# First tile of the norm after a sandwich norm made by VectorE from three prepared tiles, with six filler products in place of ten

## The reference

```python
def rmsnorm(x, gain):
    xf = x.astype(jnp.float32)
    var = jnp.mean(xf * xf, axis=-1, keepdims=True)
    return (xf * lax.rsqrt(var + RMS_EPS) * gain.astype(jnp.float32)).astype(x.dtype)

# first block
    h = rmsnorm(x, norm_mix_pre[l])
    ...
    x = x + rmsnorm(merged @ w_out[l], norm_mix_post[l])      # site "mixpost"
    h = rmsnorm(x, norm_ffn_pre[l])                           # site "ffnpre0"
    f = conv_ffn(h, ffn_w_up[l], ffn_conv_w[l], ffn_conv_b[l], ffn_w_down[l])
    x = x + rmsnorm(f, norm_ffn_post[l])                      # site "ffnpost"
# second block
    x = x + fox_mixer(rmsnorm_2(x, fox_norm[layer]), ...)     # site "fox"
```

## Time and profile before

| what | us |
|---|---|
| median of 3 runs | 2171.79 (2171.71 to 2172.0) |
| the profiled execution | 2171.54 |
| its span, first to last instruction | 2169.7 |
| TensorE busy in the span | 2159.0 |
| VectorE, ScalarE, GpSimd busy | 1210.2, 896.0, 963.7 |

### The profile page before, as it was taken

One profiled execution on the slowest core, in us unless ns is written; L12 is line 12 of the kernel. 1 busy time (PEld: TensorE's weight loads), 2 busy tenths in 40 slices (PEclk: granted clock), 3 DMA queues, 4 the chain that ended last, 5 costly groups with the idle time before them and its releaser, 6 DMA issues.

```text
span 2169.7 us, 26119 instructions
## 1 busy us (share of the span) xinstructions
PE 2159.0 (100%) x10371; PEld 1769.6 (82%) x10374; DVE 1210.2 (56%) x1721; ACT 896.0 (41%) x1405; POOL 963.7 (44%) x741
## 2 busy tenths in 40 slices
PE   9999999999999999999999999999999999999998
PEld 6887788878888878877888888888888888888887
DVE  4975424478996127775566661177676325666511
ACT  5225522354343234675533332265444434333322
POOL 4434345555565435322554444444222254444442
PEclk9999999999999999999999999999999999999999
DMA  5222223333332323211233333322211233333332
GB/s 185 78 68 68 74 83 98 99 95 98 97 98 92 97 74 106 68 50 61 95 98 97 98 95 97 99 95 69 64 56 51 66 101 92 97 97 97 96 97 89
DMA packets 59098, 191.77 MB, mean 88 GB/s; under 512 B 6592, under 2 KB 8800, under 8 KB 58976
## 3 DMA queue, kind: packets, MB, share of 16 engines
q1 hardware_dynamic: 58976, 190.09, 28.0%
HBM read 187.96 MB, written 2.10 MB: 88 GB/s over the span
## 4 chain that ended last, share of the span: by engine, by line
PE 97%; DVE 1%; DMA 1%; ACT 1%; issue 0%; POOL 0%; SPq 0%; DVEq 0%; ACTq 0%
PE ps L621 27%; PE ps L623 27%; PE ps L622 27%; PE ps L1213 2%; PE ps L1080 2%; PE ps L1089 1%; PE ps L710 1%; PE ps L711 1%; PE ps L712 1%; PE ps L1117 1%; PE ps L1166 1%; PE ps L802 1%; DMA RAW<-weights 1%; PE ps L870 0%; PE ps L739 0%
## 5 line engine op out<-in xcount | busy, mean ns | idle before, releaser
L613 POOL TENSOR_TENSOR WLO<-RAW,WHI 128x512 fp32r<-128x512 f32 (+1 forms) x723 | 956.2, 1348 | 1170.4 <-ACT WHI L1330 1167.5
L1330 ACT ACTIVATE WHI<-RAW 128x1024 fp32r<-128x1024 f32 (+3 forms) x379 | 374.0, 989 | 667.9 <-DMA RAW<-weights 470.9
L621 PE MATMUL ps<-HH,WHI 128*128 128x512 f32 x1178 | 464.6, 394 | 0.5 <-POOL WLO L613 0.5
L622 PE MATMUL ps<-HL,WHI 128*128 128x512 f32 x1178 | 458.7, 389 | 0.0
L623 PE MATMUL ps<-HH,WLO 128*128 128x512 f32 x1178 | 458.6, 389 | 0.0
L1810 DVE SCALAR_TENSOR_TENSOR CV<-U,PAR,CV 128x512 f32<-128x512 f32 x264 | 300.3, 1154 | 27.3 <-ACT CV L1579 22.2
L621 PEld LDWEIGHTS ps<-HH,WHI 128*128 128x128 f32 x1178 | 221.2, 188 | 50.5 <-issue 3.1
L622 PEld LDWEIGHTS ps<-HL,WHI 128*128 128x128 f32 x1178 | 221.2, 188 | 47.0 <-issue 2.2
L623 PEld LDWEIGHTS ps<-HH,WLO 128*128 128x128 f32 x1178 | 221.1, 188 | 46.6
L621 PE MATMUL ps<-ACTH,WHI 128*128 128x512 f32 (+1 forms) x550 | 209.4, 381 | 0.0
L622 PE MATMUL ps<-ACTL,WHI 128*128 128x512 f32 (+1 forms) x550 | 209.3, 381 | 0.0
(11 more groups left out here) (361 smaller groups left out, 3280.0 us busy)
## 6 DMA issues: line engine op xcount, KB each, us to landing
RAW<-weights SPq DMA_DIRECT2D x288, 512.0 KB, 3.5
RAW<-weights SPq DMA_DIRECT2D x56, 384.0 KB, 3.0
RAW<-weights SPq DMA_DIRECT2D x29, 256.0 KB, 2.6
RAW<-weights SPq DMA_DIRECT2D x8, 320.0 KB, 2.9
outT<-X SPq DMA_DIRECT2D x8, 256.0 KB, 2.5
X<-xT SPq DMA_DIRECT2D x3, 512.0 KB, 8.9
X<-xT SPq DMA_DIRECT2D x2, 256.0 KB, 3.2
RESET<-resets SPq DMA_DIRECT2D x1, 512.0 KB, 9.1
```

Source lines behind the costliest of these rows:

```text
L613: pool.tensor_tensor(WLO[:, slot, w], RAW[:, slot, w], WHI[:, slot, w].bitcast(F32), ALU.subtract).then_inc(w_lo, 1)
L621: pe.matmul(out, wh, hh, start=first, stop=False)
L622: pe.matmul(out, wh, hl, start=False, stop=False)
L1330: act.activation(WHI[:, slot, 0:cols], RAW[:, slot, 0:cols], ACT.Copy).then_inc(w_hi, 1)
```

## The change

Four new tiles named AHEAD (SCALED, OLD_H, ADDED_H, FIRST_H) are used at the two sandwich norms, whose products are named wout and down0.

- ScalarE, after it has squared tile 0 of wout or of down0 (`first_ahead`): SCALED = FB tile 0 times the post-norm's gain, OLD_H = X tile 0 times the next norm's gain, ADDED_H = SCALED times the next norm's gain.
- VectorE, once the token factor is in PSUM: FIRST_H = ADDED_H times the factor; HH tile 0 = OLD_H + FIRST_H; the same sum once more unrounded into ADDED_H; HL tile 0 = ADDED_H minus HH tile 0. Then tile 1 is scaled and added to X, SCALED is multiplied by the factor, and HL tile 1 made. X tile 0 is completed only then (X += SCALED).
- ScalarE makes HH for tiles 1 to 7 alone (`new_tiles`), and squares X tile 0 after HH tile 1.
- TensorE runs six filler products at the end of `token_stats` in place of ten.

```diff
-                keep_clock(6, 10)
+                keep_clock(6, 6)
...
+            def first_ahead(site, nxt):
+
+                at = 3 * SITES_BY_TOKEN.index(site)
+                act.activation(AHEAD[:, SCALED, :], tile(FB, 0), ACT.Copy, scale=par(site, 0)).then_inc(ahead, 1)
+                act.activation(AHEAD[:, OLD_H, :], tile(X, 0), ACT.Copy, scale=par(nxt, 0)).then_inc(ahead, 1)
+                act.wait_ge(ahead, at + 1)
+                act.activation(AHEAD[:, ADDED_H, :], AHEAD[:, SCALED, :], ACT.Copy, scale=par(nxt, 0)).then_inc(ahead, 1)
+
+            def new_tiles(done, nxt, between):
+
+                for j in range(1, KD):
+                    act.wait_ge(x_done, done + (1 if j == 1 else j + 1))
+                    apart()
+                    act.activation(H[0][j], tile(X, j), ACT.Copy, scale=par(nxt, j)).then_inc(h_hi, 1)
+                    if j == 1:
+                        act.wait_ge(x_done, done + 2)
+                        square(0, 0, tile(X, 0), nxt)
+                    square(j, j % 2, tile(X, j), nxt)
+                    between(j)
...
                 clear_sum(nxt)
+                dve.wait_ge(ahead, 3 * at + 3)
                 scale_known(site)
...
-                def added(j):
-                    dve.wait_ge(post_dve, j + (done + 1))
-                    dve.tensor_tensor(tile(X, j), tile(X, j), tile(FB, j), ALU.add).then_inc(x_done, 1)
-
-                scaled(0)
-                added(0)
+                def added(j, source, scaled_before):
+                    dve.wait_ge(post_dve, done + scaled_before)
+                    dve.tensor_tensor(tile(X, j), tile(X, j), source, ALU.add).then_inc(x_done, 1)
+
+                mul(AHEAD[:, FIRST_H, :], AHEAD[:, ADDED_H, :], ps[:, 7, :]).then_inc(first_h, 1)
+                dve.wait_ge(first_h, 2 * at + 1)
+                dve.tensor_tensor(H[0][0], AHEAD[:, OLD_H, :], AHEAD[:, FIRST_H, :], ALU.add).then_inc(h_hi, 1)
+                dve.tensor_tensor(AHEAD[:, ADDED_H, :], AHEAD[:, OLD_H, :], AHEAD[:, FIRST_H, :], ALU.add).then_inc(first_h, 1)
+                dve.wait_ge(h_hi, HH_AT[nxt] + 1)
+                dve.wait_ge(first_h, 2 * at + 2)
+                dve.tensor_tensor(H[1][0], AHEAD[:, ADDED_H, :], H[0][0].bitcast(F32), ALU.subtract).then_inc(h_lo, 1)
                 scaled(1)
-                for j in range(KD):
+                added(1, tile(FB, 1), 1)
+                mul(AHEAD[:, SCALED, :], AHEAD[:, SCALED, :], ps[:, 7, :]).then_inc(post_dve, 1)
+                for j in range(1, KD):
                     lo_tile(j, nxt, nxt)
+                    if j == 1:
+                        added(0, AHEAD[:, SCALED, :], 2)
+                        scaled(2)
                     if j + 1 < KD:
-                        added(j + 1)
+                        added(j + 1, tile(FB, j + 1), j + 2)
                     if j + 2 < KD:
                         scaled(j + 2)
+                    if j == 1:
+                        add_square(0, 0, nxt)
                     add_square(j, j % 2, nxt)
```

More of the change, by code:

```diff
@@ L351, in on_chip_model @@
         FB = nc.alloc_sbuf_tensor_at("FB", [P, KD, T], F32, offset=hh_at)
+        AHEAD = nc.alloc_sbuf_tensor_at("AHEAD", [P, 4, T], F32, offset=hh_at + (KD + 4) * T * 4)
+        SCALED, OLD_H, ADDED_H, FIRST_H = 0, 1, 2, 3
+        NEXT_SITE = {"mixpost": "ffnpre0", "ffnpost": "fox"}
         ffn = Region(arena)
@@ L466, in on_chip_model @@
         tap, conv_done, act_done, ffn_dve, acts = (sem(n) for n in ("tap", "conv_done", "act_done", "ffn_dve", "acts"))
-        post_dve = sem("post_dve")
+        post_dve, ahead, first_h = sem("post_dve"), sem("ahead"), sem("first_h")
         a_s, a_m, a_e, a_p, a_t, a_pt, a_o, a_hi, a_rs = (
@@ L1378, in fb_square @@
                     square(j, j % 2, tile(FB, j), site)
+                    if j == 0:
+                        first_ahead(site, NEXT_SITE[site])
                     if j == KD - 2:
@@ L1555, in _, with low_gates @@
             deviation("mixpost", D, 6)
-            for j in range(KD):
-                act.wait_ge(x_done, j + 1)
-                h_tile(j, j % 2, "ffnpre0", "ffnpre0")
+            def low_gates(j):
                 if 2 <= j < KD - 1:
                     casts(chunk_of("gate0.0", j + 1))
+            new_tiles(0, "ffnpre0", low_gates)
             casts(chunk_of("gate0.3"))
@@ L1593, in _, with forget_gates @@
             deviation("ffnpost", D, 6)
-            for j in range(KD):
-                act.wait_ge(x_done, j + (KD + 1))
-                h_tile(j, j % 2, "fox", "fox")
+            def forget_gates(j):
                 if 2 <= j < KD - 1:
                     casts(chunk_of("foxf", j + 1))
+            new_tiles(KD, "fox", forget_gates)
             casts(chunk_of("fv1.0", 1))
@@ L2163, in post_norm @@
             def post_norm(site, nxt, done):
+                at = SITES_BY_TOKEN.index(site)
                 dve.wait_ge(ln_done, STAT_AT[site] + 1)
```

## The result

The changed kernel takes 2175.50 us (median of 21 runs, 2173.93 to 2177.08) against 2171.74 for the kernel before (21 runs, 2170.55 to 2173.54): 3.76 us more. The ratio is 1.0017, with a 95% interval of 1.0011 to 1.0022. The prediction had +1.9. Its profiled execution took 2175.16, with a span of 2173.4.

What follows compares the result with a forecast made beforehand. TensorE was taken to bound the kernel (97% of the last chain). A 0.19 us gain at ffnpre0 and a 2.13 cost at fox sum to +1.94; against 2171.79 that forecast 2173.7 us, range 2171.2 to 2175.2.

Steps and rivals of the forecast that it cites:

- the chain: Whole kernel: 97% of the chain that ended last is TensorE, so a change is worth what it moves TensorE's starts.
- the first products: Both sites: TensorE's first product comes 1.57 us after VectorE's first instruction behind the token factor, 0.90 earlier.
- HL tile 1: Both sites: ends 5.77 us after VectorE's first instruction behind the token factor, 0.15 later than before at fox.
- HL tile 2: Both sites: ends 10.40 us after VectorE's first instruction behind the token factor, 2.25 later than before.
- TensorE at fox: At fox: tile 1 0.15 later, tile 2 1.52 later, tile 6, with least slack, 2.13 later; cost 2.13 us.
- TensorE at ffnpre0: At ffnpre0: start 0.90 earlier, tile 1 held to 0.73 earlier, tile 2 to 0.19 earlier; gain 0.19 us.
- So the later HL tiles stay 2.25 late: VectorE, both sites: behind HL tile 2 the order is the old one, so the delay stays 2.25 us.
- So it still finds it done, by 0.3 us: At ffnpre0: TensorE's sum over SUMSQ still finds VectorE's last addition done, with 0.3 us to spare.
- Nothing behind the norm waits for anything that was late already: Behind fox: TensorE stays as late as the 2.13 us, with no further wait.
- The predicted gain of 0.19: At ffnpre0: what the early first product leaves at tile 2, 0.19 us faster.
- the second: Rival: GpSimd hits more VectorE additions, 1.1 us each; one or two more at fox give 2174.8 to 2175.9; chance 0.13.
- The third: Rival: the granted clock falls at fox as TensorE idles before tiles 1 and 2; 6.5 us more, 2180; chance 0.04.

Runs made afterwards that it cites:

- ten_fillers: The changed kernel with ten filler products in place of six at both sites; its trace has 366.68 us from ffnpre0's t0 to fox's.
- ffnpre0_only: The change at ffnpre0 alone, with the order before and ten fillers at fox; 1.58 us over the kernel before.
- x0_behind_3: The changed kernel with SCALED's multiplication and X tile 0 moved behind HL tile 3, tile 0's square and sum behind tile 4's; +5.66 us over the kernel before.
- early_tiles: The new first tile at ffnpre0 alone, tiles 1 and 2 made earlier, the first SUMSQ addition taking two squares; +2.96 us over the kernel before.
- two_squares_out: The changed kernel without the squares of tiles 6 and 7 and their additions at ffnpre0; +1.87 us over the kernel before.
- early_psum: New first tile at ffnpre0 alone, tiles 1 and 2 earlier, running sum of squares in PSUM; +0.10 us over the kernel before, -0.28 when repeated.

## Why the prediction was wrong

**Right:** the chain, the durations and the first products (t0 + 1.56 at both sites), HL tile 1 (5.83 against 5.77), HL tile 2 (10.53 against 10.40), and the whole of *TensorE at fox* in kind and size (2.13 predicted, 2.27 at tile 6, 2.40 at the drain into FV). The wait for HL at tile 1 eats the early start there, as it said.

**The step that failed is *TensorE at ffnpre0*,** in two sentences. "So the later HL tiles stay 2.25 late" took the pace of the kernel before for granted, and with it some 2.5 us for a tile's four instructions on VectorE; from HL tile 2 on, the kernel before takes 3.0 to 3.6, as additions there are hit already (and 4.08 less 2.5 would give a slack of 1.6, not the 0.8 that stands there). The 2.25 was near: to HL tile 5 it held (2.37), and then hits by GpSimd made it 2.98 and, at the last addition, 3.52. "So it still finds it done, by 0.3 us" rested on it: the sum came at t0 + 29.85, 0.6 after TensorE was there. With the 2.37 alone it would have come at 28.70 and been in time, as it was in ten_fillers. A margin of 0.3 stood against a price of 1.1 for one hit, and the prediction carried such hits as a rival for fox alone.

**What I missed:** that casts which wait for transfers pace GpSimd. A later ScalarE finds its transfers landed, and GpSimd's pieces run back to back into VectorE's last instructions. "Nothing behind the norm waits for anything that was late already" was said of fox, where it roughly held; at ffnpre0 I didn't ask, and the wait for a bank (0.48) came on top. It is there in the two traces whose sum was 0.6 late (the changed kernel and ffnpre0_only) and in none whose sum was in time, but not in x0_behind_3 and early_tiles either, whose sum was over 2 us late; that it follows from the late sum is likely, not shown.

**The predicted gain of 0.19 was 0,** by two_squares_out. At ffnpre0 the 0.90 of the early first product shrank to 0.68 at tile 1 and 0.06 at tile 2, waiting for HL; at fox it was gone at tile 1.

**The rivals:** of the second, the mechanism came, at the other site. The third stayed away from both sites of the changed kernel, but a wait of 2.2 us at ffnpre0 in x0_behind_3 shows that it was not to be dismissed on the end of the kernel alone. In the profiled execution the miss is thus the 1.72 + 0.19 at ffnpre0, and there it is shown. That the same 1.8 us make up the miss of the median is likely, not shown: the timed runs of fox alone are as slow (+3.86 and +3.19) as those of both sites (+3.76), ffnpre0 alone is at +1.58, and each is known to within 2 us only.

## What to carry to other kernels

When instructions are added to an engine that feeds the bottleneck, follow the delay to the last consumer of that stage, not only to the first tiles, and hold every margin against the largest hit seen there: 0.3 us of slack is none where one collision costs 1.1. A delay changes who waits for transfers, and so when the other engines collide; ask what pauses in the old trace came from a transfer. Here, moving added work within a saturated engine only moved the wait; what paid at ffnpre0 was to take operands off SBUF.

## What the runs showed of the hardware

At the two sites of the fourteen traces, 316 VectorE additions and subtractions of two SBUF operands (128x512) began while no GpSimd piece ran; all took 0.68 to 0.69 us, also the 98 in which a piece began. Of 153 that began while a piece ran, 137 took 0.81 to 1.79. So an addition was hit only where the piece had begun first; in ten_fillers the last addition was ahead of the piece by 0.18 us. With the running sum in PSUM an addition took 0.68 to 0.69, all six times in early_psum, five of them begun while a piece ran. The granted clock fell to 0.50 after a single idle time of 2.20 us at ffnpre0, 1.5 us after work had begun again, and stayed there some 3 us; after 2.06 us of idle time at the same place in the profiled execution of early_tiles it stayed at 1.00 (windows from 468 to 475). Its timed runs leave open whether it did so each time: the mean granted clock is 1.000 in the five shortest and 0.999 in the six longest. The Trainium skill, "TensorE: Matmul & The Clock Gate", section "HAM oscillation — how this bites in real kernels", describes such falls behind longer waits than the one here; the measurement decides, and what told the two executions apart is open. A kernel's way between two fixed places 366.6 us apart repeated within 0.04 us over six traces, while the timed runs of one kernel spread over 3 (2170.55 to 2173.54).
